# Starting the first two weight slabs on unscaled turned rows, with the input slab first

## The reference, cut to what matters

```python
def rms_norm(x, gain):
    y = xf * lax.rsqrt(jnp.mean(xf * xf, axis=-1, keepdims=True) + EPS)
    return (y * gain.astype(jnp.float32)).astype(x.dtype)

def even_mixer(xn, pos, lb, w_in, hgrn_gain, w_out):
    h = jnp.einsum('bsd,de->bse', xn, w_in)
    aq, af, ai, bq, bk, bv, z = jnp.split(h, splits, axis=-1)
    oa = hgrn2_chunked(heads(aq), heads(af), heads(ai), lb...)   # q, forget logit f, input i
    ...

# inside hgrn2_chunked
    f = lbb + (1.0 - lbb) * jax.nn.sigmoid(to_chunks(f_logit))
    k = 1.0 - f
    b = jnp.cumsum(jnp.log(f), axis=3)
    q_dec = qc * jnp.exp(b)
    k_inv = k * jnp.exp(-b)
```

## Time and profile before

| | |
|---|---|
| time, 3 executions | 583.11 us median (581.97 to 583.24) |
| the profiled execution | 581.78 us, span 579.8 us |
| PE busy | 571.3 us, 99% of the span |
| DVE busy | 435.5 us, 75% |
| ACT busy | 392.5 us, 68% |
| POOL busy | 72.0 us, 12% |
| granted TensorE clock | 0.999 of full speed |

### The profile page before, as it was taken

The page is one execution under the profiler, slowest core; times in us unless marked ns, Lnnn a source line. Parts: engine busy times, 40 slices in busy tenths (PEclk is TensorE's granted clock), DMA queues, the critical chain, the costliest instruction groups (busy, mean ns, idle before and its releaser), DMA issues.

```text
span 579.8 us, 8803 instructions
## 1 busy us (share of the span) xinstructions
PE 571.3 (99%) x3364; PEld 504.6 (87%) x3364; DVE 435.5 (75%) x683; ACT 392.5 (68%) x600; POOL 72.0 (12%) x77
## 2 busy tenths in 40 slices
PE   8999999999999999999999999999999999999995
PEld 7999989888888888888888889999889988888984
DVE  6879689688847874568757896799998974876663
ACT  6863784596657575557666858969759837566754
POOL 4130005039101000100000001111110100100002
PEclk9999999999999999999999999999999999999999
DMA  9856355556953544564345545326544563356201
GB/s 292 257 181 229 102 189 194 170 159 193 272 167 100 200 146 145 185 230 167 145 146 167 196 158 203 122 102 235 199 146 146 182 234 139 116 204 231 93 1 73
DMA packets 51854, 98.82 MB, mean 170 GB/s; under 512 B 1733, under 2 KB 7141, under 8 KB 51813
## 3 DMA queue, kind: packets, MB, share of 16 engines
q1 hardware_dynamic: 50628, 96.95, 49.1%
q0 software_dynamic: 1024, 1.05, 0.8%
q10 hardware_dynamic: 160, 0.27, 0.1%
HBM read 96.16 MB, written 1.05 MB: 168 GB/s over the span
## 4 chain that ended last, share of the span: by engine, by line
PE 97%; DMA 1%; DVE 1%; ACT 0%; issue 0%; SPq 0%; DVEq 0%; ACTq 0%
PE proj L1972 18%; PE proj L1996 11%; PE proj L1997 11%; PE proj L1998 11%; PE proj L1973 9%; PE proj L1955 6%; PE proj L1957 6%; PE proj L1956 6%; PE head L2212 4%; PE proj L1977 3%; PE proj L1976 1%; PE head L2290 1%; PE head L2056 1%; DMA x_residual<-in_x_dram 1%; PE head L2189 1%; PE head L2257 1%
## 5 line engine op out<-in xcount | busy, mean ns | idle before, releaser
L1177 DVE TENSOR_TENSOR w_lo<-raw_weights,w_hi 128x1024 fp32r<-128x1024 f32 x174 | 222.1, 1288 | 86.8 <-ACT w_hi L548 83.1
L548 ACT ACTIVATE w_hi<-raw_weights 128x1024 fp32r<-128x1024 f32 x174 | 182.4, 1056 | 109.4 <-PE proj L1998 48.9
L1972 PE MATMUL proj<-xT,w_hi 128*128 128x512 f32 x392 | 142.0, 401 | 0.0
L1973 PE MATMUL proj<-xT,w_lo 128*128 128x256 f32 x392 | 109.8, 280 | 0.0
L1955 PE MATMUL proj<-xT,w_hi 128*128 128x256 f32 x304 | 87.3, 287 | 0.0
L1972 PEld LDWEIGHTS proj<-xT,w_hi 128*128 128x128 f32 x392 | 73.7, 188 | 15.4
L1957 PE MATMUL proj<-xT,w_lo 128*128 128x256 f32 x304 | 86.0, 283 | 0.0
L1956 PE MATMUL proj<-xT,w_hi 128*128 128x256 f32 x304 | 86.0, 283 | 0.0
L1973 PEld LDWEIGHTS proj<-xT,w_lo 128*128 128x128 f32 x392 | 74.0, 189 | 1.8
L1996 PE MATMUL proj<-w_hi,y 128*128 128x512 f32 x176 | 69.4, 395 | 0.0
L1998 PE MATMUL proj<-w_lo,y 128*128 128x512 f32 x176 | 68.6, 390 | 0.0
(11 more groups left out here) (328 smaller groups left out, 920.4 us busy)
## 6 DMA issues: line engine op xcount, KB each, us to landing
raw_weights<-in_ev_w_in_dram SPq DMA_DIRECT2D x15, 2048.0 KB, 9.1
raw_weights<-in_od_w_in_dram SPq DMA_DIRECT2D x12, 2048.0 KB, 7.9
raw_weights<-in_ev_w_out_dram SPq DMA_DIRECT2D x4, 2048.0 KB, 7.8
raw_weights<-in_xa_wkv_dram SPq DMA_DIRECT2D x4, 2048.0 KB, 8.3
raw_weights<-in_od_w_out_dram SPq DMA_DIRECT2D x4, 2048.0 KB, 7.8
raw_weights<-in_xa_wq_dram SPq DMA_DIRECT2D x2, 2048.0 KB, 9.1
raw_weights<-in_xa_wo_dram SPq DMA_DIRECT2D x2, 2048.0 KB, 7.7
x_residual<-in_x_dram SPq DMA_DIRECT2D x2, 512.0 KB, 3.9
```

The lines of the kernel that those rows point to most:

```text
L548: act.activation(ring_quarter(w_hi, n, q), raw_quarter(n, q), ACT.Copy).then_inc(hi_ready, 1)
L1177: dve.tensor_tensor(ring_quarter(w_lo, n, q), raw_quarter(n, q), ring_quarter(w_hi, n, q).bitcast(F32), ALU.subtract).then_inc(lo_ready, 1)
L1972: pe.matmul(both, wh[:, k, :], x[:, :, k, :], start=(k == 0), stop=False)
L1973: pe.matmul(dst[:, 0:S], wl[:, k, :], x[:, 0, k, :], start=False, stop=False)
```

## The change

It computes the same. (1) The slab order of group 0 becomes i, f, q, z. (2) TensorE turns the rows of x as they land, without the token factor; ACT and DVE split them into `y_hi` and `y_lo` with the gain (`raw_high`, `raw_low`), and slabs i and f of group 0 are multiplied with these unscaled rows. (3) The token factors are brought onto all partitions by two small products with a diagonal (`factor_diag`, `row_factors`); ACT applies them to i when it copies the result (scale of the copy), DVE to f's logits (`scaled_logits`). (4) For the later slabs the scaled rows are made by DVE (`normed_rows`, eight instructions), their high part by ACT (`normed_high`), their low part by POOL (two subtractions of 128x1024). (5) The four later products of ones are dropped. (6) Slab i is loaded row block by row block, slab f in four quarters. The first quarter's high part is made by POOL (blocks 0 and 1), DVE (blocks 2 and 3). (7) `angles` is cut in two: the last four instructions come after `sum_z(z, 0)`, and ACT's sine after them.

```diff
 SLABS = []
+SLABS += [("A", "i", "T", 0), ("A", "f", "F", 0), ("A", "q", "F", 0), ("A", "z", "X", 0)]
...
+        row_factors = W[:, 5, 0:S]
+        factor_diag = W[:, 4, 0:T * P].rearrange("p (t c) -> p t c", t=T)
+        x_normed = W[:, 2:4, :].rearrange("p a b -> p (a b)").rearrange("p (k t) -> p k t", k=KC)
...
@@ gpsimd
+            for k in range(2):
+                pool.wait_ge(first_landed[k], 16)
+                pool.tensor_copy(first_rows(w_hi, k), raw_quarter(0, 0)[:, k, :])
+                pool.drain().then_inc(first_hi[k], 1)
             pool.tensor_tensor(ring_quarter(w_lo, 0, 0), raw_quarter(0, 0), ring_quarter(w_hi, 0, 0).bitcast(F32),
-                               ALU.subtract).then_inc(first_lo, 1)
+                               ALU.subtract).then_inc(first_lo[0], 1)
...
+            for j in range(2):
+                pool.wait_ge(xT_hi_ready, 4 * j + 4)
+                pool.tensor_tensor(xT_lo[:, 4 * j:4 * j + 4, :], x_normed[:, 4 * j:4 * j + 4, :],
+                                   xT_hi[:, 4 * j:4 * j + 4, :].bitcast(F32), ALU.subtract).then_inc(xT_lo_ready, 4)
@@ scalar
+            raw_high(range(0, 6))
             row_squares(1, 1024)
...
+            raw_high(range(6, 8))
             ahead(-1, 3)
+            act.wait_ge(factors_psum, 1)
+            act.activation(row_factors, proj[3][:, 0:S], ACT.Copy).then_inc(factors_ready, 1)
+            ahead(i0, 0)
+            ahead(i0, 1)
+            ahead(i0, 2)
+            normed_high(0)
+            for t in range(T):
+                filled(act, i0, t)
+                act.activation(v_sb[:, t, :], bank(i0, t)[:], ACT.Copy, scale=st[:, 6 + t:7 + t]).then_inc(v_ready, 1)
...
+            ahead(i0, 3)
             act.wait_ge(lb_max, 1)
             act.activation(lbp[:, 0:3, :], lbp[:, 0:3, :], ACT.Exp).then_inc(lb_exp, 1)
+            normed_high(1)
+            ahead(slab("A", "f", 0), 0)
             act.wait_ge(soft_abs, 1)
@@ vector
+            raw_low(range(0, 4))
+            first_high(2)
+            raw_low([4])
+            first_high(3)
...
+            raw_low(range(5, 8))
             ahead(-1, 3)
-            ahead(slab("A", "f", 0), 0)
+            dve.wait_ge(factors_ready, 1)
+            normed_rows([0, 1])
+            ahead(i0, 0)
+            normed_rows([2, 3])
+            ahead(i0, 1)
+            normed_rows([4, 5])
+            ahead(i0, 2)
+            normed_rows([6, 7])
...
+            def scaled_logits(n, u):
+                filled(dve, n, u)
+                dve.tensor_tensor(blocks(0)[:, 2 * u:2 * u + 2, :], bank(n, u)..., row_factors..., ALU.mult
+                                  ).then_inc(f_scaled, 1)
...
+                if g == 0:
+                    folded_angles()
                 ahead(z, 3)
@@ tensor
-            warm_up(4)
...
+                for k in range(4):
+                    pe.wait_ge(first_hi[k], 1)
+                    pe.wait_ge(raw_lo_ready, k + 1)
+                    for t in range(T):
+                        tok = slice(P * t, P * t + P)
+                        pe.matmul(bank(n, t)[:], y_hi[:, k, tok], first_rows(w_hi, k), start=(k == 0), stop=False)
+                        pe.matmul(bank(n, t)[:], y_lo[:, k, tok], first_rows(w_hi, k), start=False, stop=False)
...
+                pe.wait_ge(diag_ready, 1)
+                for t in range(T):
+                    last = pe.matmul(proj[3][:, P * t:P * t + P], v_sb[:, 0, 0:P], factor_diag[:, t, :],
+                                     start=True, stop=True)
...
+                    first_slab(i)
+                    pe.wait_ge(prm_ready, 1)
+                    slab_f(f, [0, 1], x=(y_hi, y_lo))
+                    pe.wait_ge(factors_ready, 1)
+                    pe.wait_ge(prm_ready, 2)
+                    slab_f(f, [2, 3], x=(y_hi, y_lo))
+                    pe.wait_ge(xT_lo_ready, KC)
```

More of the change, by code:

```diff
@@ L184, in hybrid_trunk @@
         trig_ready = sem("trig_ready")
[L185 removed]
+        first_lo = [sem(f"first_lo{q}") for q in range(2)]
         eps_filled = sem("eps_filled")
@@ L635, in _, with raw_high, normed_high @@
             act.preload_act_table(ACT.Sqrt)
+            def raw_high(ks):
+                for k in ks:
+                    if k < 4:
+                        act.wait_ge(turned, k + 1)
+                    else:
+                        act.wait_ge(raw_lo_ready, k - 3)
+                    act.activation(y_hi[:, k, :], turned_at(k), ACT.Copy, scale=param("ev_norm", k)
+                                   ).then_inc(raw_hi_ready, 1)
+            def normed_high(j):
+                act.wait_ge(rows_normed, j + 1)
+                act.activation(xT_hi[:, 4 * j:4 * j + 4, :], x_normed[:, 4 * j:4 * j + 4, :], ACT.Copy
+                               ).then_inc(xT_hi_ready, 4)
             row_squares(0, 512)
@@ L700, in stage_a @@
                     rstd_a(0)
-                ahead(i, 2)
-                ahead(i, 3)
+                    ahead(i, 2)
+                    ahead(i, 3)
+                else:
+                    act.wait_ge(prm_turned, 3)
+                    act.activation(prm[:, N_EARLY:], head[0][:, N_EARLY:N_ROWS], ACT.Copy).then_inc(prm_ready, 1)
+                    ahead(q, 1)
                 act.wait_ge(b_ready, g + 1)
@@ L718, in stage_a @@
                 ahead(z, 1)
+                ahead(z, 2)
+                z_half(z, 0)
                 if g == 0:
@@ L1403, in stage_a @@
                     sign_trig()
-                ahead(f, 1)
-                ahead(f, 2)
-                forget(g, 0)
-                ahead(f, 3)
-                ahead(i, 0)
+                    ahead(f, 1)
+                    ahead(f, 2)
+                    forget(g, 0)
+                    ahead(f, 3)
+                    ahead(i, 0)
+                else:
+                    scaled_logits(f, 0)
+                    ahead(f, 1)
+                    forget(g, 0)
+                    ahead(f, 2)
+                    scaled_logits(f, 1)
+                    ahead(f, 3)
                 forget(g, 1)
@@ L1429, in stage_a @@
                     gated_a(0)
-                ahead(i, 3)
+                    ahead(i, 3)
+                else:
+                    ahead(q, 1)
                 dve.wait_ge(exps_ready, 3 * g + 3)
                 dve.tensor_tensor(wview(0), wview(1), wview(0), ALU.mult).then_inc(kinv_ready, 1)
-                ahead(q, 0)
-                ahead(q, 1)
+                if g:
+                    ahead(q, 0)
+                    ahead(q, 1)
                 ahead(q, 2)
@@ L2115, in second_quarter_products @@
-            def second_quarter_products(n):
-                pe.wait_ge(hi_ready, 2)
-                dst = bank(n, 0)[:, S:2 * S]
-                wh, wl = ring_quarter(w_hi, n, 1), ring_quarter(w_lo, n, 1)
-                for k in range(KC):
-                    pe.matmul(dst, wh[:, k, :], xT_hi[:, k, :], start=(k == 0), stop=False)
-                    pe.matmul(dst, wh[:, k, :], xT_lo[:, k, :], start=False, stop=False)
-                pe.wait_ge(lo_ready, 2)
-                for k in range(KC):
-                    last = pe.matmul(dst, wl[:, k, :], xT_hi[:, k, :], start=False, stop=(k == KC - 1))
-                last.then_inc(quarter_used, 1)
```

217 lines of the change are left out of this document (111 added, 106 removed).

## The result

The changed kernel takes 585.88 us (median of 6, 585.56 to 587.08), the kernel before in the same comparison 582.54 (581.90 to 583.24): ratio 1.0063, 95% interval 1.0052 to 1.0075, that is 3.7 us slower (3.0 to 4.4). The forecast was 586.0. The six executions of the kernel before are three at 581.90 to 581.97 and three at 583.11 to 583.24, so that its median lies where none of them does; against the lower three the changed kernel is 4.0 slower. The profiled execution took 586.08 us with a span of 584.3, 4.5 more than the span before; from the attention products of group 1 to the end the two programs take 479.2 and 479.5 us, so 4.2 of the 4.5 lie in the first 105 us.

A forecast was written before the change was run, and what follows sets the result against it. DVE, closely ahead of TensorE in the first 67 us and held by POOL, was taken to decide; 581.78 + 2.9 = 584.7 for the profiled execution, which lies 1.33 below the median of 583.11, gave 586.0, range 581.6 to 587.3.

The forecast's parts named there:

- First product: TensorE's first product of real data: at 7.3 instead of 9.61, since scaled rows no longer precede the turning.
- Hold 1: First slab: POOL's block 1 low part holds DVE's copy of block 2; TensorE waits 1.5, then 0.6 for quarter 2.
- Hold 2: Slab f's end: POOL's normed-row subtractions hold a DVE conversion and small operations; TensorE waits 1.0 at f's last conversion.
- POOL's carried factors: Behind the second qdec, they fall on DVE's: 2.93 from there to the next conversion.
- Angles and square wait: End of group 0: angles ready at 64.3, sine ahead of conversion and squares; mean of squares done 69.6 or 69.7, against 66.72.
- the sum of 4.7 for DVE: DVE's work from block 2's copy, done 10.6, through the conversion of quarter 2, at 15.3.
- 2.9 late: Mean of squares in group 0, 69.6 or 69.7 against 66.72; added to the kernel's time.
- No hold: Rival: no hold at the copies or small operations; second qdec at about 45.5, 582 to 584.3 us; chance 0.21.
- worse: Rival: slab f's quarters land late, so its conversions wait another 1.5; 587.5 us or more; chance 0.06.
- Nothing on DVE is late: Rival: faster by 2.6, 580.5 us, decided by the second qdec starting by 44; chance 0.17.
- the gain of the start: Turning begins as tile 1 of x lands, so ACT's first high part and the first product come 2.3 earlier.
- The dropped warm-up: Start: the four dropped products of ones lay in idle time and are worth nothing.

The follow-up runs named there:

- run 1: Changed kernel, but DVE instead of POOL subtracts both halves of the normed rows' low part: 585.05 us, ratio 1.0051 to the kernel before.
- run 2: Changed kernel with ACT's sine of the angles moved behind the four squares of group 0: 584.37 us, ratio 1.0039 to the kernel before.
- run 4: Changed kernel with ACT instead of DVE making the high parts of blocks 2 and 3: 585.07 us, ratio 1.0050 to the kernel before.
- run 9: As run 5, with SP issuing the 12 small loads behind slab q's load instead of ahead of it: 583.66 us, ratio 1.0029 to the kernel before.
- run 6: Run 5 plus run 2, with DVE's conversions of slab q's third and last quarters moved back: 582.22 us, ratio 1.0002 to the kernel before.
- run 5: Changed kernel with run 1 and run 4 together, and DVE also making the first quarter's low part: 584.35 us, ratio 1.0032 to the kernel before.
- run 8: Changed kernel with the four dropped products of ones back ahead of the first turning: 586.05 us, ratio 1.0063 to the kernel before.
- run 3: Changed kernel with POOL's first low part (128x1024) cut into two of 128x512: 585.58 us, ratio 1.0058 to the kernel before.

## Why the prediction was right

**The place and the mechanism of each wait** were as put down. First product 7.3 forecast, 7.37 measured. Hold 1: a copy of 2 us or more and a wait of 1.5 (2.58 and 1.46), then 0.6 before the third quarter (0.67). DVE is through the eight normed rows and three conversions, one of them held by POOL, at 23.8 (24.2). Hold 2: a wait of 1.0 (1.00). POOL's carried factors: 2.93 from the second qdec to the next conversion (2.98, against 2.13 in the kernel before); no run undoes this one. Angles and square wait: present. Runs 1, 2 and 4 take away the wait at f's last quarter, the one at the means and the one for block 2. The waits at the third quarter and at the attention products stay or grow in them (1.11 in run 4, 0.95 in run 1). Undoing POOL's subtractions, DVE's copies and slab q's late load (run 9) gives 2.55 back at the slab behind the means, and the sine's place (run 2) 1.72, 4.27 together where 4.21 were lost. That is a sum over two runs; no run has just these edits together, and run 6, which has all of them but the load's place, and two moved conversions besides, gives 3.5 back.

**The sizes were short.** The held copy ended at 10.9 instead of 10.6, the sum of 4.7 for DVE behind it measured 4.95, and the steps from there to TensorE and through two quarters took 0.3 more. That put slab f's start at 21.8 instead of 21.0, f's last conversion at 30.33 instead of 29.6 and the scan at 39.81 instead of 38.6; from there every step stays 1.2 to 1.3 behind its forecast: kinv 45.54 (44.3), second qdec 49.56 (48.3), attention products 50.34 (49.1), angles ready 65.6 (64.3), slab behind the means 70.93 (69.65). The term "2.9 late" measured 4.2 between the two profiled executions. That the time came out within 0.2 of 586.0 all the same is luck: I took the median of before as 583.11, one of its longer executions, and in this and the later comparisons the median is 582.54 and 581.8 to 582.1. The two errors cancel. From one profiled execution to the other the forecast was 581.78 to 584.7, and it became 586.08; the loss is 3.7 between the medians and 4.3 between the profiled executions, not 2.9.

**The rivals.** "No hold" was wrong about the holds. Its price no run shows by itself: in run 5 nothing is held at the copies or the small operations, but DVE makes three low parts more; its 584.35 lies at the end of that rival's 582 to 584.3, its second qdec (48.51) 3.0 behind the rival's 45.5, and part of that was the landing of slab q. I had looked for a late landing in slab f's quarters (rival "worse"), where no wait appeared. It was the next slab that came late, behind twelve small loads which in turn stood behind the four issues of these quarters, 7.5 us on SP; run 9 tests the small loads' place, and no run the four issues. "Nothing on DVE is late" asked for a second qdec by 44. With slab q early and without the holds up to there it starts at 47.02 (run 9), but with three low parts of 1.2 more on DVE and two copies less, so this too speaks against the rival without settling it. How full DVE is stands in the table of windows, 12 to 48 us (length; busy us of PE, its loads, DVE, ACT, POOL), of before, of the changed kernel and of run 9:

```profile
12.00:48.00 36.00, 36.00 (x248) 33.27 (x247) 29.18 (x44) 24.52 (x30) 10.59 (x15) 1.00 0.73 235
```

```profile
12.00:48.00 36.00, 34.32 (x244) 31.84 (x243) 33.26 (x53) 25.05 (x31) 10.80 (x13) 1.00 0.76 230
```

```profile
12.00:48.00 36.00, 34.20 (x246) 31.71 (x246) 32.42 (x55) 27.16 (x33) 6.53 (x9) 1.00 0.77 227
```

DVE was busy for 29.2 of 36 us and is now for 33.3, of which 4.0 are the two holds beside L467 (2.96 and 2.38 instead of 1.22 and 0.17). Run 9's 32.4 are without them, but two low parts of POOL's (2.4) are in them. The three also do not get equally far in 36 us. From 12 us to its second qdec DVE is busy for 26.9 of 33.5 in the kernel before, 34.8 of 37.6 in the changed one and 31.7 of 35.0 in run 9. In the changed kernel the stretch grows by 4.1, which is what the two holds cost, while the rest of the added work (the normed rows are 3.5 of it, the scaled logits 1.4) fills most of the time in which DVE used to wait. In run 9 the attention products start at 47.80, as in the kernel before (47.95), although TensorE started 2.2 earlier. So the gain of the start is spent there on normed rows, scaled logits and low parts, and in the changed kernel the holds and the sine are lost on top. The dropped warm-up was worth nothing, as costed (run 8).

## What to carry to other kernels

Before giving work to POOL, read what DVE does at that moment: a subtraction of 128x1024 on SBUF operands there costs a busy DVE up to its whole duration of 2.4 us (1.7 to 2.2 measured in the changed kernel) if DVE comes to a copy or to an operation on two SBUF operands meanwhile, where DVE would have made it in 1.2; cut in pieces it costs the piece that DVE meets. An earlier start of TensorE is worth only what the engine next to it has to spare: count that engine's busy time in the stretch, with the new work, before the start. When an activation is made to wait longer, move it behind what does not need it; and when a stall is mended, look at the landing and the issue queue behind it before expecting the whole of it back.

## What the runs showed of the hardware

- A one-input copy of 128x512 and additions of eight columns are held just as conversions are: 2.58 instead of 0.41, and 2.38 instead of 0.17. The Trainium skill ("SBUF — State Buffer", section "Who interferes with whom") has the rule; the trace agrees, by run 3 too, where the hold shortened with the piece (1.51 and 1.11) and an operation with a PSUM input passed in 0.47. The prediction had expected both holds.
- Four loads of 512 KB in rows of 512 bytes kept SP for 7.2 to 7.5 us, where the next load of 2 MB in rows of 2 KB took it 0.37 (run 9). The length of the rows does not explain this by itself: the kernel before issued two loads of the same shape in 1.05 together, at 1.72, when the DMA engines had just started (busy share 0.17 in the first 2 us), and its small load of ev_hgrn_gain took 2.06 at 8.53, where it took 0.48 at 16.63 in run 9. How much was under way differs as well, and no run separates the two. In this kernel the price fell on a slab that is not theirs.
- In run 5 TensorE stood still for 2.58 us, and from about 49.9 to 53.3 its granted clock was half of full speed (the lower of its two levels, 1.2 GHz). It is the only profiled execution here in which the clock fell ahead of the last 5 us; the waits behind the first product in the other kernels, of up to 1.5, were not followed by a fall.
